# A decoder trunk on eight cores: three factors of the pool branch multiplied once on the chip

## The reference, cut to what matters

```python
h = rmsnorm(x, pre_mix_g[i])
proj = h @ w_in[i] + b_in[i]
z = proj[..., :POOL_WIDTH]
...
mixed = jnp.einsum('bsgc,gcd->bsgd', pooled, pool_w)
pool = mixed.reshape(B, S, POOL_WIDTH) * pool_scale
...
ya = pool_mixer(z, pool_w[i], pool_scale[i]) @ w_pa[i]
yb = sgu_mixer(u, v, ...) @ w_pb[i]
merged = gates[:, :, 0] * ya + gates[:, :, 1] * yb
x = x + rmsnorm(merged @ w_o[i], post_mix_g[i])
```

## Time and profile before

| what | value |
|---|---|
| median of 3 runs | 2176.4 us |
| the profiled execution's own time | 2177.32 us |
| its span on the slowest core (core 2) | 2175.4 us |
| spans of the eight cores | 2170.3 to 2175.4 us |
| mean granted TensorE clock | 0.989 to 0.990 on all cores |
| TensorE busy | 2075.9 us of the span |

### The profile page before, as it was taken

One profiled execution on the slowest core, in us unless ns is written; L12 is line 12 of the kernel. 1 busy time (PEld: TensorE's weight loads), 2 busy tenths in 40 slices (PEclk: granted clock), 3 DMA queues, 4 the chain that ended last, 5 costly groups with the idle time before them and its releaser, 6 DMA issues.

```text
span 2175.4 us, 30026 instructions; the slowest of 8 cores (2170.3 to 2175.4 us)
## 1 busy us (share of the span) xinstructions
PE 2075.9 (95%) x10640; PEld 1043.8 (48%) x10818; DVE 1016.7 (47%) x1607; ACT 848.1 (39%) x1344; POOL 82.1 (4%) x156
## 2 busy tenths in 40 slices
PE   2999999999899999999989999999999999999996
PEld 1546666676544444444434444444444344444442
DVE  2438555302673856430374565541066385553027
ACT  2345154312645307321374522631166451543125
POOL 0000000000000000000000000000000000000000
PEclk8999999999999999999999999999999999999998
DMA  8234454434444363455576453554343344445342
GB/s 188 41 50 77 75 82 69 72 65 68 89 77 64 53 97 59 74 92 78 106 171 159 67 87 60 85 90 78 59 82 64 63 84 78 78 69 90 56 78 78
DMA packets 36325, 176.82 MB, mean 81 GB/s; under 512 B 3282, under 2 KB 6482, under 8 KB 18770
## 3 DMA queue, kind: packets, MB, share of 16 engines
q0 software_dynamic: 22912, 148.92, 42.6%
q1 hardware_dynamic: 13268, 25.98, 4.0%
HBM read 315.40 MB, written 8.39 MB: 149 GB/s over the span
## 4 chain that ended last, share of the span: by engine, by line
PE 92%; DMA 3%; ACT 2%; issue 2%; DVE 1%; SPq 0%; DVEq 0%; ACTq 0%; POOLq 0%
PE PS L676 80%; PE PS L794 5%; PE PS L593 3%; DMA XB<-xT 2%; PE PS L798 1%; PE PS L898 1%; PE PS L1108 1%; DMA WB<-wst 1%; PE PS L881 1%; ACT L1098 0%; PE PS L565 0%; ACT TMP L1098 0%; DVE U0A L906 0%; DVE XB L994 0%; ACT U1B L635 0%
## 5 line engine op out<-in xcount | busy, mean ns | idle before, releaser
L676 PE MATMUL PS<-U0A,WB 128*128 128x512 bf16 (+2 forms) x2907 | 525.5, 338 | 51.8 <-ACT U3A L833 22.6
L676 PE MATMUL PS<-U0B,WB 128*128 128x512 bf16 x2252 | 503.1, 379 | 3.1 <-ACT U56B L737 0.4
L676 PEld LDWEIGHTS PS<-U0A,WB 128*128 128x128 bf16 x2944 | 289.6, 99 | 271.4 <-issue 60.7
L676 PEld LDWEIGHTS PS<-U0B,WB 128*128 128x128 bf16 x2304 | 224.0, 98 | 264.2 <-issue 1.4
L1024 ACT ACTIVATE TMP<-PS 128x512 f32<-128x512 f32 (+1 forms) x256 | 151.3, 598 | 250.2 <-PE PS L676 245.4
L952 ACT ACTIVATE U1A<-PS 128x512 bf16<-128x512 f32 (+1 forms) x64 | 37.3, 603 | 391.6 <-PE PS L676 391.6
L487 POOL DMA_DIRECT2D WB<-wst x144 | 76.3, 530 | 2028.4 <-PE PS L676 1580.2
L676 PE MATMUL PS<-U2A,WB 128*128 128x512 bf16 (+1 forms) x631 | 120.5, 337 | 0.5
L676 PE MATMUL PS<-U3A,WB 128*128 128x512 bf16 (+1 forms) x637 | 118.0, 338 | 0.2
L676 PE MATMUL PS<-U2B,WB 128*128 128x512 bf16 x498 | 116.8, 379 | 0.9
L676 PE MATMUL PS<-U3B,WB 128*128 128x512 bf16 x504 | 117.1, 379 | 0.4
(11 more groups left out here) (184 smaller groups left out, 2242.1 us busy)
## 6 DMA issues: line engine op xcount, KB each, us to landing
WB<-wst POOLq DMA_DIRECT2D x136, 1024.0 KB, 10.8
XB<-xT SPq DMA_DIRECT2D x2, 2048.0 KB, 37.6
WB<-wst POOLq DMA_DIRECT2D x8, 512.0 KB, 6.3
outT<-XA SPq DMA_DIRECT2D x16, 256.0 KB, 2.9
outT<-XB SPq DMA_DIRECT2D x16, 256.0 KB, 6.9
XA<-xT SPq DMA_DIRECT2D x4, 528.0 KB, 9.4
U2A<-wsT SPq DMA_DIRECT2D x4, 512.0 KB, 6.2
BF<-bsbc SPq DMA_DIRECT2D x4, 512.0 KB, 7.0
```

The costliest lines, as they stand in the source:

```text
L676: return lambda e: e.matmul(PS[:, bk, 0:w], WB[:, b, k * kstride + fi * 128: k * kstride + (fi + 1) * 128], rhs(k, c0, c0 + w), start=(k = ...
```

## The change

Because the three factors are linear, their product is made once per layer on the chip, by a new function `fold`, while the first pair of tiles (`st == 0`) runs. `fold` scales the `pool_w` block in place (8 instructions on VectorE), multiplies it with the two halves of `w_pa` (32 matmuls a layer, TensorE), and writes the product back over the `w_pa` blocks in the ring (VectorE and ScalarE in turn). SP stores both to device memory (`wfold`, bfloat16, 1 MB each). `pm_stage` is gone: `pa_half` reads U1 with the folded block, in all tiles. For the second pair (`st == 1`) the `pool_w` block isn't loaded and `wfold` is loaded in place of `w_pa`. `pool_w` is transposed on the host. The steps around it have a new order: `gb_half(1)` of A, the fold, `gb_half(1)` of B, both `pa_half` of A, both of B, then `pb_half(0)` of A and B.

```diff
+        stream = [(st, l, j) for st in range(NTILE // 2) for l in range(L) for j in range(NBLK)
+                  if st == 0 or j != SHORT_POOLW]
...
+            if st > 0 and j in (SHORT_POOLW + 1, SHORT_POOLW + 2):
+                h = j - SHORT_POOLW - 1
+                P.dma("pool", "w%d" % b, lambda e: e.dma_start(out=WB[:, b, :], in_=wfold[l, h]), 0.9 * n,
+                      reads=list(behind) + [rFD[l][h]], writes=[rW[b]])
...
-            def pm_stage(self, b4):
...
-                yield from self.fm(blk, self.h, self.rh, 8, evac, perk=(half == 0))
+                yield from self.fm(blk, lambda k, c0, c1: S.u(1, k, c0, c1),
+                                   lambda k: [S.rU[1][k], rFB[half][k // 2]], 8, evac, perk=(half == 0))
...
+        def fold(l, bp, bs):
+
+            for i in range(8):
+                w = WB[:, bp, i * 256:(i + 1) * 256]
+                P.op("dve", dve_ns(256, False, 2), lambda e, w=w, i=i: e.tensor_scalar(
+                    out=w, in0=w, scalar1=cv(l, V_PSCALE, i), scalar2=None, op0=ALU.mult),
+                    reads=[rW[bp], rC], writes=[rW[bp]])
+            for half in range(2):
+                b = bs[half]
+                for g in range(4):
+                    bk = banks(2) if psn[0] < 7 else banks(2)
+                    for cc in range(2):
+                        fns = [lambda e, dc=dc, cc=cc, g=g, b=b, bk=bk: e.matmul(
+                            PS[:, bk[cc], :], WB[:, bp, (g * 2 + dc) * 256 + cc * 128:(g * 2 + dc) * 256 + cc * 128 + 128],
+                            WB[:, b, (g * 2 + dc) * 512:(g * 2 + dc + 1) * 512], start=(dc == 0), stop=(dc == 1))
+                            for dc in range(2)]
+                        P.group(fns, 2 * 512 * NS_COL, reads=[rW[bp], rW[b], rFB[half][g]], writes=[rPS[bk[cc]]])
+                    for cc in range(2):
+                        k = g * 2 + cc
+                        out = WB[:, b, k * 512:(k + 1) * 512]
+                        if cc:
+                            P.op("act", act_ns(512, True), lambda e, out=out, bk=bk: e.activation(
+                                out=out, in_=PS[:, bk[1], :], func=AF.Copy), reads=[rPS[bk[1]]], writes=[rFB[half][g]])
+                        else:
+                            P.op("dve", dve_ns(512, True), lambda e, out=out, bk=bk: e.tensor_copy(
+                                out=out, in_=PS[:, bk[0], :]), reads=[rPS[bk[0]]], writes=[rFB[half][g]])
+                P.dma("sp", "fo%d%d" % (l, half), lambda e, half=half, b=b: e.dma_start(out=wfold[l, half], in_=WB[:, b, :]), 4000.0,
+                      reads=rFB[half] + [rW[b]], writes=[rFD[l][half]])
...
-                both(3, lambda T, w: [T.gb_half(w[0], 1), T.pm_stage(w[1]), T.pa_half(w[2], 0)])
-                both(2, lambda T, w: [T.pa_half(w[0], 1), T.pb_half(w[1], 0)])
+                if st == 0:
+                    bs = w_take(4)
+                    run([A.gb_half(bs[0], 1)])
+                    fold(l, bs[1], bs[2:])
+                    run([B.gb_half(bs[0], 1)])
+                    w_done(B.S)
+                    bs = bs[2:]
+                else:
+                    bs = w_take(1)
+                    run([A.gb_half(bs[0], 1)])
+                    run([B.gb_half(bs[0], 1)])
+                    bs = w_take(2)
+                run([A.pa_half(bs[0], 0), A.pa_half(bs[1], 1)])
+                run([B.pa_half(bs[0], 0), B.pa_half(bs[1], 1)])
+                both(1, lambda T, w: [T.pb_half(w[0], 0)])
```

More of the change, by code:

```diff
@@ L333, in build_nc @@
     outT = nc.dram_tensor("outT", [128, 8, OWN], F32, kind="ExternalOutput").ap()
+    wfold = nc.dram_tensor("wfold", [L, 2, 128, BLK], BF16, kind="Internal").ap()
     P = Prog()
@@ L362, in build_nc @@
         PS = es.enter_context(nc.psum_tensor("PS", [128, 8, 512], F32))
-        for key in Prog.ENG + ("cst", "bv", "ws", "bs", "xh", "f0", "f1", "f2", "f3") + tuple("w%d" % i for i in range(NWBUF)):
+        for key in Prog.ENG + ("cst", "fo00", "fo01", "fo10", "fo11", "bv", "ws", "bs", "xh", "f0", "f1", "f2", "f3") + tuple("w%d" % i for i in range(NWBUF)):
             P.add_sem(key, es.enter_context(nc.semaphore("s_" + key)))
@@ L474, in sv @@
             return ap if len(cbl) == 1 else ap.rearrange("p (b w) -> p b w", b=2)
-        stream = [(l, j) for _ in range(NTILE // 2) for l in range(L) for j in range(NBLK)]
+        stream = [(st, l, j) for st in range(NTILE // 2) for l in range(L) for j in range(NBLK)
+                  if st == 0 or j != SHORT_POOLW]
+        rFD = [R(2) for _ in range(L)]
+        rFB = [R(4), R(4)]
         wstate = {"issued": 0, "cons": 0}
@@ L482, in w_issue @@
                 return
-            l, j = stream[i]
+            st, l, j = stream[i]
             b = i % NWBUF
             n = 2048 if j in SHORT_BLKS else BLK
+            if st > 0 and j in (SHORT_POOLW + 1, SHORT_POOLW + 2):
+                h = j - SHORT_POOLW - 1
+                P.dma("pool", "w%d" % b, lambda e: e.dma_start(out=WB[:, b, :], in_=wfold[l, h]), 0.9 * n,
+                      reads=list(behind) + [rFD[l][h]], writes=[rW[b]])
+                wstate["issued"] += 1
+                return
             P.dma("pool", "w%d" % b,
@@ L885, in sgu_head @@
                 self.sgu_gate(h, PS[:, bk, 0:512], [rPS[bk]], OWN0, COLS)
-            def pm_stage(self, b4):
-                S, l = self.S, self.l
-                a, b = self.r
-                for gi in range(8):
-                    g, dh = gi // 2, gi % 2
-                    bks = banks(len(self.cbs))
-                    fns = []
-                    for cc in range(2):
-                        for bk, (c0, w) in zip(bks, self.cbs):
-                            o0 = (g * 2 + cc) * 256 + dh * 128
-                            fns.append(lambda e, bk=bk, o0=o0, g=g, cc=cc, c0=c0, w=w: e.matmul(
-                                PS[:, bk, 0:w], WB[:, b4, o0:o0 + 128], S.u(1, 2 * g + cc, c0, c0 + w),
-                                start=(cc == 0), stop=(cc == 1)))
-                    P.group(fns, 2 * self.n * NS_COL, reads=[rW[b4], S.rU[1][2 * g], S.rU[1][2 * g + 1]],
-                            writes=[rPS[bk] for bk in bks])
-                    rp = [rPS[bk] for bk in bks]
-                    out = sv(S.u(0, gi, a, b), self.cbs)
-                    if gi % 2 == 0:
-                        P.op("dve", dve_ns(self.n, True), lambda e, bks=bks, gi=gi, out=out: e.tensor_scalar(
-                            out=out, in0=ps(bks, self.cbs), scalar1=cv(l, V_PSCALE, gi), scalar2=None, op0=ALU.mult),
-                            reads=rp + [rC], writes=[S.rU[0][gi]])
-                    else:
-                        P.op("act", act_ns(self.n, True, 1), lambda e, bks=bks, gi=gi, out=out: e.activation(
-                            out=out, in_=ps(bks, self.cbs), func=AF.Identity, scale=cv(l, V_PSCALE, gi)),
-                            reads=rp + [rC], writes=[S.rU[0][gi]])
-                    if gi % 4 == 3:
-                        yield
-                w_done(S)
             def pa_half(self, blk, half):
@@ L1293, in _build_wstream @@
             ws[l, j] = _blk_k512(w_in, c0)
-        ws[l, SHORT_POOLW, :, :2048] = inp["pool_w"][l].reshape(4, 2, 128, 256).transpose(2, 0, 1, 3).reshape(128, 2048)
+        ws[l, SHORT_POOLW, :, :2048] = inp["pool_w"][l].transpose(0, 2, 1).reshape(4, 2, 128, 256).transpose(2, 0, 1, 3).reshape(128, 2048)
         for i, name in enumerate(("w_pa", "w_pb", "w_o")):
```

## The result

| | before | after |
|---|---|---|
| time, us | 2176.4 (median when the prediction was made) | 2164.4 (median of 4: 2162.0 to 2164.9) |
| profiled execution, its own time | 2177.3 | 2164.9 |
| span of the slowest core | 2175.4 (core 2) | 2163.0 (core 0) |
| spans of the eight cores | 2170.3 to 2175.4 | 2158.9 to 2163.0 |
| matmuls recorded | 10640 | 10738 |

The account below looks back on a forecast made before the run. TensorE's queue and its few waits were taken to bound the kernel. Matmuls -28.2 + 13.8 = -14.4 us, grown waits +2.1, the rest 0: -12.3 us, forecast 2164.5 us, ratio 0.994, range 2160.5 to 2171 us.

Parts of the forecast that it names:

- The reason is the order on ScalarE, not the time on VectorE: B's gb_half(0), layer 0: the pool chunk read-out stands behind the second sigmoid output on ScalarE, so TensorE waits +1.4 us.
- pm_stage goes, -28.2, and the fold's matmuls come, +13.8: TensorE: eight pm_stage passes go, 64 fold matmuls of 216 ns come, net -14.4 us.
- Read-outs of the fold, 0: Fold: VectorE and ScalarE read out 8 banks each and keep up with TensorE; no cost, up to 2 us a layer.
- The scalings' grown waits, +2.1: B's gb_half(0): scalings push the last pool chunks back; TensorE waits +1.4 us in layer 0, +0.7 in layer 1.
- The wait for the second half of w_pa, 0: Fold's second half: block 12's load lands 0.4 us ahead of its use in each layer, so no wait.
- The order and the loads, 0: Reordered steps and the second pair's smaller loads: later loads stay hidden, fewer bytes are worth nothing.
- No grown wait: Rival, B's gb_half(0): the two ScalarE places don't bite, -14.4 us, 2162.4 us; chance 0.20.
- The second half is late: Rival, fold's second half: w_pa loads land as slowly as 13.7 us, +5.7 us, 2170.2 us; chance 0.08.
- starved: Rival, fold's second half: loads land as late as the program's first, 24.0 us, +26 us, 2190 us; chance 0.03.
- Descriptors held up: Rival, GpSimd's load queue: each scaling holds a load up for its own time, +3.2 us, 2167.7 us; chance 0.04.
- The change doesn't give what it removes: Rival, post_mix and the layers behind: the gain turns into waits further on, 2176.5 us; chance 0.04.

Follow-up runs that it names:

- version held until mid-way: Changed kernel with the fold's scalings held until the second head of B's gb_half(0) is done: 2160.7 us.
- the first experiment: Changed kernel with the fold's scalings held back until the first group of matmuls of A's gb_half(1) is done: 2163.6 us.
- the second experiment: Changed kernel with one sigmoid output of B's gb_half(0) (second in layer 0, first in layer 1) held behind B's last pool chunk on ScalarE: 2160.9 to 2164.3 us.
- the order alone: Kernel before with only the new order of steps, pm_stage and all its matmuls kept, no fold: 2174.0 to 2175.2 us.
- The fifth experiment: Changed kernel with the fold ahead of A's gb_half(1) in place of behind it: 2180.7 us.
- experiment 16: Not a separate run: the 16 counts matmuls in the run of the changed kernel with the fold ahead of A's gb_half(1), 2180.7 us.

## Why the prediction was right or wrong

**The step that failed** is the sentence "The reason is the order on ScalarE, not the time on VectorE", for layer 0. The prediction put VectorE's share in the grown wait at nothing and gave VectorE a part only in the upper bound. With ScalarE's order forced back, only 0.57 of the 1.36 us went. The other 0.79 is VectorE's order: two instructions that now stand between the head's read-out and the copy into the slot make the copy 0.80 us late. The sum came out right all the same, because in the changed kernel ScalarE's delay is the longer of the two and hides the other.

**The time**: 2164.5 forecast, 2164.4 measured, inside 2160.5 to 2171. That the two agree to 0.1 us is luck: the base was a median of three executions, and the same kernel moves by more than 1 us outside the stretches. The fair comparison is the change, -12.3 forecast and -12.06 in the stretches. The terms:

- **pm_stage goes, -28.2, and the fold's matmuls come, +13.8**: right. The fold took 6.90 us twice. The second pair's stretch fell by 6.91 us in layer 0 and 6.93 in layer 1, the 2 x 3.46 of the prediction. The version with no grown waits measures the whole term by itself, -14.37 against the -14.4 forecast. The upper bound that I had given a fold matmul (10% more, for both operands in the weight ring) didn't come into play.
- **Read-outs of the fold, 0**: right. A copy on VectorE takes 687 ns, and TensorE never waited in the changed kernel's fold, on any core; the experiment with the fold behind B's `gb_half(1)` shows it where it would have hurt most.
- **The scalings' grown waits, +2.1**: the places were right and the sum near, +1.36 and +0.96, 2.3 us in all; the version held until mid-way shows that they can be had back, and the first experiment that it is the scalings that make them. For layer 0 the chain on ScalarE is the one that was forecast, to the size (1.36), but it isn't the only one, as said above. What I had missed is that the scalings also change VectorE's own order around the copy, and that the first of them waits for `pool_w` and holds VectorE's queue; the hold costs TensorE something only where it is longest (0.2 us on one core of eight here, 0.43 on one core of the second experiment). In layer 1 the step was right: forced, 0.95 of 0.96 us went. The size of a scaling was near: 0.28 us recorded, 0.20 from one to the next, for the 0.25 taken. The size of the wait in layer 1, 0.7 for 0.96, was low because the sigmoid output ahead of the chunks started 0.3 us behind the head's start (733.28 against 732.96), where I had 0.1.
- **The wait for the second half of w_pa, 0**: right, but closer than one core shows. On core 0 the load was issued at 205.5 us and landed in 8.9, at 214.4, and the fold's second half began at 213.10 + 3.45 = 216.55: 2.1 us of slack. Over the eight cores and both layers the slack is 0.3 to 3.0 us. Landing times go by core: these loads took 8.0 to 10.7 us after, and in the trace of before 8.1 to 11.3, of which I had read the 10.3 to 10.6 of its slowest core. So 0.4 us of slack was about right for a core with slow loads, and that no core waited is in part luck. That the mechanism is there was shown by taking its cover away.
- **The order and the loads, 0**: right, shown by the order alone (0.00 us) and, for the loads, by the fold in both pairs.

**The rivals.** *No grown wait* fell by the waits in the trace. *The second half is late*, and *starved*: fell, the slack was 0.3 us or more on every core. *Descriptors held up*: the load of block 11 was issued at 196.3, among the scalings of that core, and landed in 8.8 us; block 12's, issued with one scaling left, in 8.9. A hold-up of 2 us can't be seen: over the cores the two loads took 8.0 to 10.7 us, and before, with no scalings, 8.1 to 11.3. By the rule of the Trainium skill ("SBUF — State Buffer", section "Who interferes with whom") a hold-up would last at most as long as the scalings that overlap, 0.28 us at a time, which this spread can't tell from nothing. *The change doesn't give what it removes*: fell as far as can be told. The stretches alone could not show it, since they end where this rival begins; outside them stand 1604.2 and 1602.6 us after, against 1603.1 and 1602.8 before, where this rival asks for 12 more.

One more step was loose. I wrote of a wait's price as its length. The fifth experiment shows waits on TensorE that cost more than themselves (6.6 us cost 9.1, 5.1 cost 7.3); the price of the starved fold, +26 us, was too low for that, and it would have turned the sum from a landing earlier than I gave.

## What to carry to other kernels

Where TensorE is bound by its queue, a product of constants that is made once is worth its matmuls in every later tile and costs them in the first; with two uses per core, half of the gain goes to making it. Helper instructions that are free by busy time aren't free by place: look at every queue that they stand in or reorder, and ask of the instruction that frees a buffer what now stands before it. Let the helpers stand behind it and ahead of their own deadline, and name both ends (too early cost 2.3 us here, too late 3.0, between them nothing). Where two causes overlap, taking one away shows only the difference between them; here it took both experiments, ScalarE's order alone and the scalings moved, to see the second. Read a slack on all cores, not on the slowest alone. Measure a change of some 10 us by the stretch that it touches, from one of TensorE's starts to another on all cores; here the median repeats to 0.01 us, where the whole time moves by 1 or 2. Then look outside the stretch too.

## What the runs showed of the hardware that was not expected

- **Matmuls behind a wait can run at the lower clock.** In the fifth experiment 16 matmuls took 4.8 to 6.2 us in place of 3.45 behind the long waits for a load, and full-speed time behind the short ones. It isn't only in that experiment. At the first change of layer in the changed kernel, TensorE's matmuls after a wait of 4.25 us take from 597.60 to 600.96 us for eight, 0.42 us each in place of 0.216. The last row is the granted clock of that time, with the columns as above:

```profile
597.60 3.57 PE L687 MATMUL PS<-U0A,WB 128*128 128x512 bf16 x8 [4.25 <-DVE U0A L657]
600.96 3.06 PE L604 MATMUL PS<-U1B,ONEB 128*128 128x512 bf16 x8
...
597.60:601.00 3.40, 3.40 (x9) 1.20 (x10) 3.40 (x6) 0.00 (x0) 0.00 (x0) 0.50 1.05 149
```

  The clock's two levels are 1.2 and 2.4 GHz, and this is the lower one. Behind the waits of 1.51 and 1.34 us in the same trace matmuls kept 0.216 us and the granted clock was 1.00 (201 to 203 us and 734.6 to 736.6).
- **A load that converts takes longer, and landing times go by core.** 1 MB of bfloat16 loaded from `wfold` landed in 5.1 us, 1 MB of bfloat16 made from 2 MB of float32 in 9.0 (medians of the changed kernel's core 0), and SP's stores of 1 MB to device memory in 3.9. On core 2 of the same trace the first two are 6.5 and 10.5. Whether the doubled bytes or the conversion make the difference no run shows:

```profile
WB<-wst POOLq DMA_DIRECT2D x132, 1024.0 KB, 9.0
wfold<-WB SPq DMA_DIRECT2D x4, 1024.0 KB, 3.9
WB<-wfold POOLq DMA_DIRECT2D x4, 1024.0 KB, 5.1
```

  The Trainium skill ("DMA: Bandwidth & Descriptors", section "Anatomy of one DMA — SWDGE (gpsimd) path") has some 2.0 us plus the bytes at 436 GB/s; worked out from that, an estimate is 4.4 us for 1 MB and 6.8 for 2 MB. The load of 1 MB is 0.7 us over it on core 0, the converting load 2.2 us.
